# Where a residual's scaling, a rotation's cosines and unread matmuls stand in a two-layer decoder trunk

## The reference, cut to what matters

```
h = x * (1.0 + sc1) + sh1
p = h @ w_in[l]
q, k, v, qi, ki, wi, xr, yg = jnp.split(p, split_at, axis=-1)
...
qi = apply_rope(qi.reshape(B, S, IDX_HEADS, IDX_HEAD_DIM), cos_i, sin_i)
...
mix = merged @ w_out[l]
x = layer_norm(alpha * x + (1.0 + g1) * mix, ln1_g[l], ln1_b[l])
h2 = x * (1.0 + sc2) + sh2
ff = jnp.square(jax.nn.relu(h2 @ w_up[l])) @ w_down[l]
x = layer_norm(alpha * x + (1.0 + g2) * ff, ln2_g[l], ln2_b[l])
```

## Time and profile before

| | |
|---|---|
| Time, median of 3 runs | 1346.77 us (1345.81 to 1348.87) |
| The profiled execution, own time | 1348.24 us |
| Its span, first to last instruction | 1346.3 us |
| TensorE busy | 1284.0 us, 95% |
| VectorE busy | 787.1 us, 58% |
| ScalarE busy | 555.5 us, 41% |
| GpSimd busy | 151.7 us, 11% |
| TensorE's granted clock, mean | 0.983 |
| HBM read | 155.64 MB, 117 GB/s |

### The profile page before, as it was taken

One profiled execution on the slowest core, in us unless ns is written; L12 is line 12 of the kernel. 1 busy time (PEld: TensorE's weight loads), 2 busy tenths in 40 slices (PEclk: granted clock), 3 DMA queues, 4 the chain that ended last, 5 costly groups with the idle time before them and its releaser, 6 DMA issues.

```text
span 1346.3 us, 17032 instructions
## 1 busy us (share of the span) xinstructions
PE 1284.0 (95%) x6229; PEld 1005.3 (75%) x6229; DVE 787.1 (58%) x1274; ACT 555.5 (41%) x842; POOL 151.7 (11%) x123
## 2 busy tenths in 40 slices
PE   4999998899999999999998999979999999999996
PEld 2766766687888888888876676757778888888886
DVE  2658977766743635537475698874674343433354
ACT  2753555634622313314257335573283242331331
POOL 2000334111000000000120013420200000000012
PEclk9999998999999999999998999989999999999997
DMA  9753434222353242342253444421123333333311
GB/s 315 231 185 125 157 126 146 90 78 63 110 166 100 93 156 93 99 151 94 78 173 110 137 146 141 159 91 34 62 79 120 100 93 93 93 101 102 94 63 63
DMA packets 76469, 158.56 MB, mean 118 GB/s; under 512 B 6528, under 2 KB 14968, under 8 KB 76408
## 3 DMA queue, kind: packets, MB, share of 16 engines
q1 hardware_dynamic: 64064, 112.80, 26.9%
q0 software_dynamic: 11712, 44.57, 9.9%
q10 hardware_dynamic: 632, 0.39, 0.1%
HBM read 155.64 MB, written 2.10 MB: 117 GB/s over the span
## 4 chain that ended last, share of the span: by engine, by line
PE 80%; ACT 9%; DVE 7%; issue 2%; DMA 1%; POOL 1%; POOLq 0%; ACTq 0%; SPq 0%; DVEq 0%
PE bank L646 24%; PE bank L648 23%; PE bank L647 23%; PE bank L693 2%; PE bank L611 1%; DMA first_mod<-in_w_mod_dram 1%; PE bank L545 1%; ACT w_hi L997 1%; PE bank L841 1%; ACT turned_ring L1100 1%; ACT resid L1029 1%; DVE resid L1470 1%; ACT turned_ring L1099 1%; PE bank L875 1%; DVE a_lo L1503 1%
## 5 line engine op out<-in xcount | busy, mean ns | idle before, releaser
L1461 DVE TENSOR_TENSOR w_lo<-w_raw,w_hi 128x1024 fp32r<-128x1024 f32 x168 | 206.0, 1233 | 335.3 <-ACT w_hi L997 335.3
L997 ACT ACTIVATE w_hi<-w_raw 128x1024 fp32r<-128x1024 f32 x192 | 201.5, 1057 | 465.9 <-PE bank L648 464.8
L646 PE MATMUL bank<-a_hi,w_hi 128*128 128x512 f32 x896 | 361.3, 403 | 7.9 <-ACT turned_ring L1100 5.5
L648 PE MATMUL bank<-a_hi,w_lo 128*128 128x512 f32 x896 | 350.4, 391 | 0.0
L647 PE MATMUL bank<-a_lo,w_hi 128*128 128x512 f32 x896 | 349.9, 390 | 0.0
L646 PEld LDWEIGHTS bank<-a_hi,w_hi 128*128 128x128 f32 x896 | 168.8, 188 | 68.8 <-issue 26.6
L646 PE MATMUL bank<-b_hi,w_hi 128*128 128x512 f32 x512 | 199.7, 390 | 0.0
L648 PE MATMUL bank<-b_hi,w_lo 128*128 128x512 f32 x512 | 199.2, 389 | 0.0
L647 PE MATMUL bank<-b_lo,w_hi 128*128 128x512 f32 x512 | 199.2, 389 | 0.0
L648 PEld LDWEIGHTS bank<-a_hi,w_lo 128*128 128x128 f32 x896 | 168.6, 188 | 36.6
L647 PEld LDWEIGHTS bank<-a_lo,w_hi 128*128 128x128 f32 x896 | 169.1, 189 | 34.7 <-issue 1.9
(11 more groups left out here) (254 smaller groups left out, 1421.9 us busy)
## 6 DMA issues: line engine op xcount, KB each, us to landing
mod_raw<-in_w_mod_dram POOLq DMA_DIRECT2D x40, 1024.0 KB, 5.9
w_raw<-in_w_up_dram SPq DMA_DIRECT2D x64, 512.0 KB, 3.7
w_raw<-in_w_down_dram SPq DMA_DIRECT2D x64, 512.0 KB, 3.7
w_raw<-in_w_in_dram SPq DMA_DIRECT2D x48, 512.0 KB, 3.7
first_mod<-in_w_mod_dram SPq DMA_DIRECT2D x8, 1024.0 KB, 12.9
w_raw<-in_w_out_dram SPq DMA_DIRECT2D x16, 512.0 KB, 3.8
x_in<-in_x_dram POOLq DMA_DIRECT2D x4, 512.0 KB, 10.4
out_dram<-y_out SPq DMA_DIRECT2D x8, 256.0 KB, 2.1
```

Of the source, the lines that this page charges most:

```text
L646: mm(o, wh, hi(kk), start=first, stop=False)
L648: last = mm(o, wl, hi(kk), start=False, stop=fin)
L997: last = af(hi, src, ACT.Copy)
L1461: last = tt(lo, src, hi.bitcast(F32), ALU.subtract)
```

## The change

The first part moves the scaling of layer 1 from ahead of the xr splits to four places in ScalarE's work beside the xr group, two tiles at each. The second lets VectorE write `qi_rot` as bank times cosine, all four tiles first, and then sines and sums; ScalarE copies only the swapped quarters and waits, tile by tile, for the cosine product, so that a bank is freed only after both have read it. The third puts two unread matmuls ahead of a LayerNorm's first sums and two between its second and third, and the wait for bank 6 with them to the front.

```diff
@@ layer_norm, TensorE
+                pe.wait_ge(free_s[6], uses_before(6, "down12", l, NC - 1) + 1 if tail else uses_before(6, "out12", l) + 1)
+                keep_busy(2)
                 pe.wait_ge(ln_q_s, n * (DK - 2) + 2)
                 pe.wait_ge(free_s[4], uses_before(4, "sums" + tail, l))
                 add(TT, ln_q, first=True)
-                pe.wait_ge(free_s[6], uses_before(6, "down12", l, NC - 1) + 1 if tail else uses_before(6, "out12", l) + 1)
                 keep_busy(3)
                 pe.wait_ge(ln_s_s, n)
                 add(0, ln_s)
+                keep_busy(2)
                 pe.wait_ge(ln_sq_s, n * DK)
@@ ScalarE
-            def scale_residual(blk):
-                for kk in range(DK):
+            def scale_residual(blk, tiles=range(DK)):
+                for kk in tiles:
...
-                if l:
-                    scale_residual(0)
-
...
                 def qi_out():
+                    half = IDX_DH // 2
                     for m in range(4):
-                        rope_tile("qi", qi[:, m, :], m, half=IDX_DH // 2)
+                        r = ring_of("qi", m)
+                        act.wait_ge(qi_cos, l * 4 + (m + 1))
+                        ring_free("qi", m)
+                        for at in range(0, P, 2 * half):
+                            af(ring[at:at + half, r, :], banks[m][at + half:at + 2 * half, :], ACT.Copy)
+                            last = af(ring[at + half:at + 2 * half, r, :], banks[m][at:at + half, :], ACT.Copy)
+                        last.then_inc(free_s[m], 1)
...
+                def scale_some(n):
+                    if l:
+                        scale_residual(0, range(2 * n, 2 * n + 2))
+                scale_some(0)
                 split_hi("v", l, 1)
+                scale_some(1)
                 idx_relu(1, range(0, 4))
                 split_hi("v", l, 2)
+                scale_some(2)
                 idx_relu(1, range(4, 8))
+                scale_some(3)
                 xr_out()
                 split_hi("v", l, PAIRS - 1)
@@ VectorE
+                def qi_cosine(m):
+                    ve.wait_ge(full_s[m], uses_before(m, f"qi{m}", l) + 1)
+                    tt(qi[:, m, :], banks[m][:, :], cos_i[:, :], ALU.mult).then_inc(qi_cos, 1)
+
+                def qi_sine(m):
+                    swapped = ring[:, ring_of("qi", m), :]
+                    ve.wait_ge(free_s[m], uses_before(m, f"qi{m}", l) + 1)
+                    step(tt(swapped, swapped, sin_i[:, :], ALU.mult))
+                    step.settle()
+                    ve.wait_ge(qi_cos, l * 4 + (m + 1))
+                    tt(qi[:, m, :], qi[:, m, :], swapped, ALU.add).then_inc(rope_done, 1)
+
                 def qi_out():
                     for m in range(4):
-                        rope("qi", m, qi[:, m, :], cos_i, sin_i)
+                        qi_cosine(m)
+                    for m in range(4):
+                        qi_sine(m)
```

More of the change, by code:

```diff
@@ L295, in trunk_kernel @@
         ff_sq = sem("ff_squared")
-        rope_done = sem("rope_done")
+        rope_done, qi_cos = sem("rope_done"), sem("qi_by_cosine")
         idx_acc = sem("idx_accumulated")
```

## The result

The changed kernel takes 1339.07 us, median of five runs (1337.16 to 1340.47), against 1346.77 for the kernel before in the same comparison (1345.67 to 1348.87): ratio 0.9939, with an interval of 0.9924 to 0.9955. Times 1346.77 that is 1338.55, a gain of 8.2 us where 5.7 was forecast. A second comparison, made later, gave 1340.57 and a ratio of 0.9963 (0.9949 to 0.9976), a gain of 5.0. It is faster beyond doubt; how much it gains differs by 3 us between two comparisons of the same code, and a good part of this document is about where those 3 us sit.

A forecast was written before the change was run, and what follows sets the result against it. The chain of waits was taken as the bound, TensorE holding 80% of it. Terms −6.35 + 0 + 0.67 gave −5.7 us, from the median 1346.77 to 1341.0 us, range 1338.6 to 1344.0.

The forecast's parts named there:

- Part A: Start of layer 1's xr: residual scaling moved from ahead of the splits, −6.35 us, bounds −5.0 and −6.75.
- Part B: qi take-out in both layers: fewer ScalarE instructions, given back waiting for VectorE's cosine; worth nothing, bounds +1.4 and −1.7.
- Part C: Three mid-kernel LayerNorms: four more unread matmuls each, +2.0 us, less one clock fall avoided at 1.33, net +0.67.
- The sum: Whole kernel: −6.35 + 0 + 0.67 = −5.7 us, giving 1341.0 us from the median of 1346.77.
- The price: Mid-kernel LayerNorms: the unread matmuls add 0.21 us before the first sums and 0.46 between second and third, together 0.67.
- The count of falls: Mid-kernel LayerNorms: one clock fall left of two, a fall costing 1.07 to 1.60 us, 1.33 on average.
- filler without effect: Rival at the mid-kernel LayerNorms: two or three clock falls stay despite unread matmuls, 1342.4 or 1343.8 us; chance 0.18.
- The road to the end: From the three mid-kernel LayerNorms onward: their +2.0 and −1.33 us were added whole to the final time.
- clock falls that shift by chance: Attention stages: chance shifts of clock falls were left outside the range of 1338.6 to 1344.0 us.
- The clock rule: At xr and LayerNorms: idle gaps drop the clock, so xr's fall goes and LayerNorms' falls stay, 1342.4 us.

The follow-up runs named there:

- the cosines first: On the changed kernel, VectorE makes the first two qi cosines between its weight splits instead of behind all three; ratio 0.9942 to the kernel before.
- the splits first: On the changed kernel, up1's first weight splits moved ahead of ScalarE's eight residual scalings for the second block; 1337.05 us with filler, 1335.7 without.

## Why the prediction was right or wrong

**Part A: right, in place and size.** Forecast −6.35 from xr's first matmul to its twentieth, measured 11.27 − 4.87 = 6.40; the wait left was 0.24 where I had 0.4, and the clock stayed up. Alone it gave 6.5 us. The scalings came back beside xr without a new wait, and VectorE didn't hold the gain back: from xr's first matmul to out1's last one it takes 240.90 us instead of 247.36, as much less as the first twenty matmuls, within 0.1 us.

**Part B: right.** Nothing, by 0.9995. The place was as described, ScalarE idle 2.26 us for 2.4 forecast, the cosine 0.62 us for 0.68. That the wait behind VectorE's splits is the reason is shown by the cosines first: in those seven executions TensorE's waits are gone in both layers, in six of them with no fall ahead of layer 0's.

**Part C: the step that failed.** The sum had C at "+0.67": filler at "2.0 us in three", less one fall of two at 1.33, both passed on to the end whole. In the traced pair C's three places gave +0.02, −0.57 and +0.20, together −0.35. That is 1.0 of the 2.4 us by which the traces' −8.1 passes the forecast; the last LayerNorm, which the sum put at nothing, is another 1.2, and A and the rest are 0.2. Three things were wrong in it.

The price: at full clock a LayerNorm takes 9.52 to 9.66 us without filler, 10.06 to 10.11 with both pairs, 9.62 to 9.64 with the first pair alone. So the first pair costs 0.1, not 0.21, the second 0.46 as forecast, together 0.57 and not 0.67.

The count of falls: with both pairs 5 in 21 LayerNorms (seven traced executions, all five in two of them), without 17 in 21. Falls are rarer, as argued, but the third LayerNorm's full clock in the kernel before was a chance draw: in the six other executions without filler it fell. The same code fell in none of three places or in all. A fall costs 1.0 to 2.7 us, not 1.07 to 1.60; in the second execution of the changed kernel the three made their stretches 1.48, 2.21 and 1.06 us longer than in the first, together more than the two comparisons differ. The case of the rival "filler without effect" with three falls left, 1343.8, is what the same kernel took in that execution, 1344.0.

The road to the end: I let the LayerNorms' time pass on whole. Ahead of the first MLP the wait at up1 took the saved fall up (1.03 us shorter, 0.02 gained), and in the kernel before the wait at xr did the same for the second. Part A takes that second absorber away, which ties the terms together: with the scaling moved, most of a fall in the second LayerNorm reaches the end (280.35 and 282.39 without filler, LayerNorms of 9.66 and 12.26), and before it did not (287.73 and 287.84, LayerNorms of 10.66 and 12.26). The third column therefore fell by 7.03 and not by 6.35: 6.40 at xr, 0.57 from the second LayerNorm, and 0.06 between. Ahead of the second MLP nothing took up the filler's time in the kernel with filler alone (0.57 longer, stretch 0.56); in the changed kernel 0.20 of it is seen, and where the rest went was not separated.

The remaining −1.19 lies in the last LayerNorm, where "clock falls that shift by chance" were named for the attention stages only. In the traces its stretch is 17.0 to 17.2 us in twelve executions and 17.5 to 18.3 in five, whatever the part: the change did not earn it.

The change's own gain is thus A's 6.4 and what the second LayerNorm happens to keep; a sum of −6.4 to −6.8 lies within both comparisons' intervals. That the forecast of −5.7 lies between their −8.2 and −5.0 is luck, since C's +0.67 was not found. The clock rule that I weighed at the LayerNorms, that of the Trainium skill, page TensorE: Matmul & The Clock Gate, section Why this matters for your kernels, lays drops to idle gaps between bursts of matmuls. It does not fit here: in the executions above the clock fell with TensorE busy for 12.08 of 12.08 us. At xr it fits in kind only, and less well than the prediction has it: the clock fell behind one gap, of 2.05 us, shorter than those that the page warns of, and ahead of the one of 1.80, since this matmul of the kernel before already took 0.63 us for 0.39.

```profile
723.56 0.63 PE L648 MATMUL bank<-a_hi,w_lo 128*128 128x512 f32 x1
```

## What to carry to other kernels

A place where an engine waits for another takes up what the waiting engine alone loses ahead of it, as far as the wait goes; a loss that delays the other engine too passes on. So a gain of the waiting engine just ahead of such a wait is worth nothing, and removing the wait makes the losses ahead of it count: look for the next late arrival behind each stage, and ask whether that engine is late as well, before a saving is added to a sum. Work that has a late deadline (a scaling for a residual sum) belongs behind the splits of the weights that TensorE wants next, wherever the two stand on one engine: that gave 6.4 us at xr and 1.9 at each up1. And where the clock falls in one execution and not in the next, look at several traces before a fall is booked to a cause.

## What the runs showed of the hardware

The clock fell to its lower level in LayerNorms in which TensorE was busy all the time (12.08 of 12.08 us, mean clock 0.72), among or just behind sums whose matmuls write one column. Falls were rarer with two full-width matmuls ahead of these sums and two behind the second ones: 5 of 21 LayerNorms against 17 of 21. With the first two alone (0.1 us) one fall in three places was traced, with the second two alone (0.46 us) three in three. These are one execution each, and the mean clocks of the runs (0.988 and 0.984) carry the comparison, so that it is a lead and not shown. Why the same instructions fall in one execution and not in another stayed open; no run here separates it.

The first 315 us differ between executions of equal code by 1.7 to 1.8 us in two pairs (314.90 and 313.19 in the changed kernel, 314.81 and 312.97 with the splits first), and by 3.7 with the cosines first (309.91 to 313.60, kernels that differ only behind that stretch), more than most of the parts are worth. In the changed kernel the second execution is ahead by 1.8 us already at its first qi matmul, at 31.73 instead of 33.55. What made it begin earlier was not separated.
